# A decoder layer with experts: a 21st weight buffer, and single buffers for gathered rows and for a pair's result

## What is computed

```python
g_w, g_idx = lax.top_k(g_prob, 1)
e_w, e_idx = lax.top_k(e_prob, TOP_K_IN_GROUP)
w = e_w / jnp.sum(e_w, axis=-1, keepdims=True) * g_w
for e in range(N_EXPERTS):
    h = jax.nn.silu(xt @ lp['w_e_gate'][e]) * (xt @ lp['w_e_up'][e])
    y = y + combine[:, e:e + 1] * (h @ lp['w_e_down'][e])
```

## Time and profile before

| | |
|---|---|
| median of 3 runs | 804.66 us (803.05 to 805.99) |
| the profiled execution's own time | 804.41 us |
| its span, first to last instruction | 802.3 us |
| PE busy | 757.4 us (94%) |
| DVE, ACT, POOL busy | 390.1, 244.0, 74.5 us |
| DMA | 190.64 MB, mean 238 GB/s |
| chain that ended last | PE 76%, DMA 14%, ACT 5%, DVE 3% |

### The profile page before, as it was taken

The page is one execution under the profiler, slowest core; times in us unless marked ns, Lnnn a source line. Parts: engine busy times, 40 slices in busy tenths (PEclk is TensorE's granted clock), DMA queues, the critical chain, the costliest instruction groups (busy, mean ns, idle before and its releaser), DMA issues.

```text
span 802.3 us, 12106 instructions
## 1 busy us (share of the span) xinstructions
PE 757.4 (94%) x4992; PEld 577.7 (72%) x4992; DVE 390.1 (49%) x733; ACT 244.0 (30%) x429; POOL 74.5 (9%) x104
## 2 busy tenths in 40 slices
PE   8999999999999999999999999999999997788884
PEld 6889999999998766789999989887333332333322
DVE  3599828994632747466344358446111111113227
ACT  1552333213473435553243243112111110110113
POOL 0100022001003010100000010002112112111100
PEclk9999999999999999999999999999999999999998
DMA  9668134623345454210242378269999999999995
GB/s 343 239 179 336 60 112 79 153 68 151 93 152 209 187 210 158 106 54 2 105 139 86 158 299 340 99 218 384 398 417 427 419 420 427 420 422 426 421 398 190
DMA packets 38140, 190.64 MB, mean 238 GB/s; under 512 B 5914, under 2 KB 7466, under 8 KB 21864
## 3 DMA queue, kind: packets, MB, share of 16 engines
q1 hardware_dynamic: 23696, 148.22, 46.8%
q0 software_dynamic: 11200, 34.98, 13.1%
q10 hardware_dynamic: 3184, 6.60, 2.2%
HBM read 176.17 MB, written 21.41 MB: 246 GB/s over the span
## 4 chain that ended last, share of the span: by engine, by line
PE 76%; DMA 14%; ACT 5%; DVE 3%; issue 1%; SPq 1%; DVEq 0%; ACTq 0%; POOLq 0%
PE ps L619 72%; DMA sb<-in_wexp 10%; PE ps L630 4%; DMA expert_rows<-sb 2%; DMA sb<-expert_rows 1%; ACT sb L1522 1%; ACT sb L1451 1%; DMA sb<-in_xT 1%; SPq L519 1%; ACT sb L1323 1%; ACT sr L1438 0%; DVE sb L2559 0%; ACT sb L1500 0%; DVE sb L2059 0%; DVE sr L2032 0%
## 5 line engine op out<-in xcount | busy, mean ns | idle before, releaser
L619 PE MATMUL ps<-sb 128*64 128x512 f32 (+15 forms) x2208 | 383.4, 434 | 29.2 <-DMA sb<-in_wexp 17.9
L619 PE MATMUL ps<-sr 128*128 128x288 f32 (+2 forms) x2378 | 337.0, 302 | 3.5 <-DVE sr L2502 1.6
L619 PEld LDWEIGHTS ps<-sb 128*64 128x64 f32 (+6 forms) x2208 | 217.9, 157 | 167.4 <-issue 130.1
L619 PEld LDWEIGHTS ps<-sr 128*128 128x128 f32 x2378 | 319.9, 188 | 15.8 <-issue 5.1
L630 PEld LDWEIGHTS ps<-sb 128*128 128x128 f32 (+3 forms) x406 | 41.8, 140 | 32.1 <-issue 28.9
L2428 DVE SCALAR_TENSOR_TENSOR sb<-sb,ps 128x256 f32<-128x256 f32 x16 | 6.7, 421 | 116.6 <-ACT sb L1690 116.6
L630 PE MATMUL ps<-sb 128*128 128x128 f32 (+3 forms) x406 | 52.9, 269 | 3.3 <-issue 1.7
L2167 DVE TENSOR_TENSOR sr<-sb,sr 128x2048 fp32r<-128x2048 f32 (+1 forms) x15 | 34.7, 2324 | 27.4 <-ACT sr L1433 17.6
L2436 DVE COPY sb<-ps 128x1024 f32<-128x1024 f32 x15 | 18.4, 1225 | 57.6 <-PE ps L619 57.6
L1323 ACT ACTIVATE sb<-ps 128x576 f32<-128x576 f32 (+4 forms) x29 | 22.9, 790 | 70.3 <-PE ps L619 50.4
L2153 DVE SCALAR_TENSOR_TENSOR sb<-sb,ps 128x576 f32<-128x576 f32 x24 | 18.1, 753 | 53.3 <-PE ps L619 53.3
(11 more groups left out here) (279 smaller groups left out, 482.7 us busy)
## 6 DMA issues: line engine op xcount, KB each, us to landing
sb<-in_wexp SPq DMA_DIRECT2D x91, 1024.0 KB, 22.0
sb<-in_wstream SPq DMA_DIRECT2D x33, 1024.0 KB, 5.3
expert_rows<-sb ACTq DMA_DIRECT2D x1, 4608.0 KB, 20.1
sb<-in_mkT POOLq DMA_DIRECT2D x8, 512.0 KB, 8.8
sb<-in_mv POOLq DMA_DIRECT2D x8, 512.0 KB, 6.4
sb<-expert_rows SPq DMA_DIRECT2D x4, 1024.0 KB, 9.5
sb<-in_wexp SPq DMA_DIRECT2D x5, 768.0 KB, 24.9
sb<-in_x SPq DMA_DIRECT2D x4, 512.0 KB, 14.4
```

What stands on the lines that cost most here:

```text
L619: return signed(nc.tensor.matmul(*a, **kw))
```

## The change

1. **A 21st slot.** It is put in ahead of the last one and has two pieces of half a chunk each, so a chunk that goes there is two transfers: `M_YO + 1024`, until now the second result buffer, and `M_XG + 1024`, until now the second buffer of gathered rows. Chunk n goes to slot n modulo 21; from chunk 21 on it waits for chunk n - 21. Since an odd number of slots no longer falls into pairs, the semaphores are a ring of their own (`EW_RING`, 11).
2. **Order on SP.** Chunk 19, now in the new slot, is started behind chunk 18 and before the wait for the stores of `xn2_rows`; it waits for logits of the fourth row block (`lg3`), which have read the place before. Chunk 20 goes behind that wait.
3. **One buffer of gathered rows.** gather(i) waits until turn_rows(i-1) is done, where before it waited for turn_rows(i-2).
4. **One result buffer.** result(i) waits until scatter(i-1) has landed, where before it waited for scatter(i-2).
5. **The last result.** `L_HI` and `L_SEL` move to the places of slots 13 and 12. ACT drops its wait for a scatter, DVE's wait for turned rows becomes one for `ew_used`.

```diff
-SLOTS_E += [straight(O_X)]
+SLOTS_E += [[(M_YO + 1024, ((1, 1024),), 0, 1024), (M_XG + 1024, ((1, 1024),), 1024, 1024)], straight(O_X)]
+EW_RING = 11
 def landed(n):
 
-    k = n % NSLOT // 2 * 2
-    return 16 * (len(SLOTS_E[k]) + len(SLOTS_E[k + 1])) * (n // NSLOT + 1)
+    pairs = range(n // 2 % EW_RING, n // 2 + 1, EW_RING)
+    return 16 * sum(len(SLOTS_E[2 * m % NSLOT]) + len(SLOTS_E[(2 * m + 1) % NSLOT]) for m in pairs)
...
-L_HI, L_LO, L_SEL, L_W = M_YO + 1024, M_XGT, M_XG + 1024, R_SS + 13
+L_HI, L_LO, L_SEL, L_W = SLOTS_E[13][0][0], M_XGT, SLOTS_E[12][0][0], R_SS + 13
...
-                    sp.dma_start(at(off, *dims), src).then_inc(ew_ready[n % NSLOT // 2], 16)
+                    sp.dma_start(at(off, *dims), src).then_inc(ew_ready[n // 2 % EW_RING], 16)
...
             for n in range(15, 19):
                 main_chunk(n)
+            filled(sp, f"lg{TT - 2}")
+            main_chunk(19)
             sp.wait_ge(x2_out[0], 48)
             sp.wait_ge(x2_out[1], 32)
-            for n in range(19, N_MAIN):
+            for n in range(20, N_MAIN):
                 wait_pos(sp, ew_used, n + 1 - NSLOT)
...
-                    last = turn_tile(pat(0, kt * 128, (1, 128)), at(M_XG + (i % 2) * 1024 + kt * 128, (1, 128)), ident)
+                    last = turn_tile(pat(0, kt * 128, (1, 128)), at(M_XG + kt * 128, (1, 128)), ident)
...
             act.wait_ge(slot_oh, 3)
-            act.wait_ge(y_sent[1], 16 * (NPAIR // 2 - 1))
...
                 dve.wait_ge(y_ps, i + 1)
-                wait_pos(dve, y_sent[i % 2], 16 * (i // 2))
-                v.tensor_copy(at(M_YO + (i % 2) * 1024, (1, 1024)), pat(3, 0, (1, 1024))).then_inc(y_copied, 1)
+                if i:
+                    dve.wait_ge(y_sent[(i - 1) % 2], 16 * ((i + 1) // 2))
+                v.tensor_copy(at(M_YO, (1, 1024)), pat(3, 0, (1, 1024))).then_inc(y_copied, 1)
...
-                dve.wait_ge(xt_ps, NPAIR)
+                dve.wait_ge(ew_used, N_MAIN - NSLOT + 2)
...
-                wait_pos(pool, xt_ps, i - 1)
+                if i > 1:
+                    pool.wait_ge(xt_ps, i)
                 pool.indirect_dma_start(
-                    out=at(M_XG + (i % 2) * 1024, (1, D)), out_offset=None, in_=x2_d[:, :],
+                    out=at(M_XG, (1, D)), out_offset=None, in_=x2_d[:, :],
```

More of the change, by code:

```diff
@@ L163 @@
 SLOTS_E += [straight(a) for b in (0, 2) for a in (raw_at(NBLOCKS - 4 + b), raw_at(NBLOCKS - 3 + b), HI_AT["w", b], HI_AT["w", b + 1])]
-SLOTS_E += [straight(O_X)]
+SLOTS_E += [[(M_YO + 1024, ((1, 1024),), 0, 1024), (M_XG + 1024, ((1, 1024),), 1024, 1024)], straight(O_X)]
 NSLOT = len(SLOTS_E)
-assert NSLOT == 20 and O_XH + 3584 <= WORDS and O_X + 4096 <= O_TH
+EW_RING = 11
+assert NSLOT == 21 and NSLOT <= 2 * EW_RING - 1 and O_XH + 3584 <= WORDS and O_X + 4096 <= O_TH
 def piece_of(n, i):
@@ L420, in build @@
         x2_out = [sem(f"x2_out{i}") for i in range(2)]
-        ew_ready = [sem(f"ew_ready{i}") for i in range(NSLOT // 2)]
+        ew_ready = [sem(f"ew_ready{i}") for i in range(EW_RING)]
         ew_used = sem("ew_used")
@@ L573, in _ @@
                 sp.wait_ge(added, 1)
+                sp.wait_ge(y_lo, 2)
                 for n in range(N_MAIN, len(CHUNKS)):
@@ L1116, in weights_of @@
                 if n % 2 == 0:
-                    pe.wait_ge(ew_ready[n % NSLOT // 2], landed(n))
+                    pe.wait_ge(ew_ready[n // 2 % EW_RING], landed(n))
                 return n
@@ L2683, in scatter @@
                     out=y_d[:, :], out_offset=bass.IndirectOffsetOnAxis(at(M_IDX + i, (1, 1)).bitcast(U32), 0),
-                    in_=at(M_YO + (i % 2) * 1024, (1, D)), in_offset=None,
+                    in_=at(M_YO, (1, D)), in_offset=None,
                     bounds_check=PAIRS - 1, oob_is_err=False).then_inc(y_sent[i % 2], 16)
```

## The result

The changed kernel takes 807.14 us as a median of 22 runs (806.07 to 812.76), the kernel before 804.64 us in as many on the same chip. The ratio is 1.0035 with a 95% interval from 1.0026 to 1.0044: **slower, by 2.5 us between the medians and 2.8 us by the ratio**, where 0.9 us less was forecast, and above the range's end of 806.8. The profiled execution takes 807.03 us (span 805.2).

What follows compares the result with a forecast made beforehand. The stream of weights was taken to bound the kernel. The slot's -2.0 us and the result buffer's +1.1 us, with nothing for the other parts, gave -0.9 us: from 804.66 to 803.8 us, range 802.0 to 806.8.

Steps and rivals of the forecast that it cites:

- Part 1, the slot: Chunk 19 starts near 542 us and fills the DMA hole at 555 to 570 us: gain 2.0 us (1.3 to 2.5).
- bytes or busy share: Two measures of the hole at 555 to 570 us: missing bytes give 2.7 us, the DMA engines' empty share 1.3.
- Part 2, the rows: At the experts' start, turn_rows(1) and (2) come 2.0 and 3.1 us later, hidden by queued weights; the end not later.
- The cover: At the experts' start, about 3.5 us remain before the weights' queue runs dry, against a PE delay of 3.1 us.
- Part 3, the result buffer: At the end, result(14) waits for scatter(13), 5.6 us later, so the loads of the results end 1.1 us later.
- (a): At the end, scatter(14) starts loaded and ends alone: 5.0 us, landing at 775.1.
- (b): Behind scatter(14), the first load of the results, 1024 KB alone, takes 4.8 us instead of 6.4, landing at 779.9.
- (c): From the landing of scatter(14), a chain without slack runs to the end; no change in its length was forecast.
- The rival on the slower side: At the end, scatter(14) is as slow as under load, deciding from 5.9 us: +1.9 us, 806.6 or 807.3; chance 0.15.
- That rows bind: Rival: the single buffer of rows costs PE 3.1 us at the start or up to 12.8: 806.9 to 816.6; chance 0.05.
- That the tail is free: Rival: at the end scatter(14) lands within about 3.9 us, so loads wait for DMA alone: 802.4 us; chance 0.18.
- Released after 776: Sign of error at the end: the loads of the results are released after 776 us.

Runs made afterwards that it cites:

- the two experiments without the slot: Kernel before with one result buffer alone: 809.31 us, ratio 1.0057; kernel before with one buffer of gathered rows alone: 804.35 us, ratio 1.000.
- the kernel with the own place: Changed kernel, but result(14) goes to a place of its own in a used weight slot, without waiting: 802.94 us, ratio 0.9968; again 802.61 and 802.83 us.
- the last experiment: Six spare products on PE before turn_rows(1), added to the kernel with the own place: 806.09 us, ratio 1.0026.

## Why the prediction was wrong

- **Part 1, the slot: right, in mechanism and about in size.** The step taken as 2.0 measured 2.5 in the profiled execution, in two more of the changed kernel 1.4 and 2.9. The last is more than one chunk can give, so these marks move by themselves; the two experiments without the slot have 200.8 and 201.3 in place of 201.6. The medians of the kernel with the own place, which keeps the slot and the single buffer of rows, give 1.5 to 1.8 us: 2.0 was rather a little high, and whether bytes or busy share (1.3) was the better measure stays open.
- **Part 2, the rows: right in sum, the steps differ from execution to execution.** Late by 2 and 3 us was forecast, 0 and 0.9 came in the profiled execution, and alone the single buffer changed nothing (ratio 1.000). Gather(2) landed after 8.7 us, as forecast (8.8), but gather(1) in at most 6.1 (turn_rows(1) stands that far behind it), so that the delay did not begin with it. In the ten profiled executions with the early chunk 19 and nothing else changed at this place, turn_rows(1) came 7.0 to 10.2 us after the first product, where it was 7.4 before: the 2.0 us happen, but not always. The cover, taken as some 3.5 us, is rather 2 by the last experiment. What the single buffer costs beside the slot, where gathers meet a full queue, no run shows by itself.
- **Part 3, the result buffer: the right place, three sizes off, all to the same side. This is the step that failed.** (a) scatter(14) was to start loaded and end alone, 5.0 us; it took 6.44, on DMA engines that moved 14 GB/s at the end. A free queue did not make it fast: its last packets were late although little else was under way. By the fit of the Trainium skill (DMA: Bandwidth & Descriptors, Anatomy of one DMA — SWDGE (gpsimd) path) 3.2 us would have done, as an estimate; the fastest scatter(14) in any run, by the time from its start to the loads that wait for it, took 5.9. (b) The first load was to take 4.8 us alone, because the 6.4 of before were put down to the last chunk ahead of it. With nothing ahead of it, it took 6.2, and 6.1 to 6.3 in the nine other profiled executions with a late result(14). The row it was priced by the earlier trace rows is a transfer with none behind it; behind the first load come four more, and the engines had moved some 1.9 MB when its 1.05 had landed. That this is what made it late is argued; no run started it alone. With result(14) late by 5.3 us in place of 5.6, these two are 2.6 us. (c) "From there a chain without slack runs to the end" was taken as a chain of unchanged length. It grew by 2.3 us in the profiled execution, by 1.1 and 2.5 in two more of the changed kernel, since weights that came earlier and loads that came later left PE idle, and at half clock around and behind that.
- **The rival on the slower side** had the place right, and a scatter(14) above the 5.9 us from which it was to decide, though not as slow as under load. It was given 0.15 because "half of its time falls after the last weights". That its price, 3.9 us, is near the 3.7 that came by the landing of the first load is luck: it was made of a scatter of 7.8 us and a load of 4.8, where 6.44 and 6.2 were measured. So is the time near its 807.3, which had a gain of 1.3 us in it and no longer end. **That rows bind** fell as the cause of the loss: ratio 1.000 alone, and the loss is gone with the own place, which keeps the single buffer of rows. **That the tail is free** fell with the 6.44 us. The rule of two buffers (the Trainium skill, Trainium Kernel Development and Optimization, Best Practices) is borne out at the results, 4.7 us, and not at the rows.
- **Released after 776** was named as a sign of error; the release came at 773.3, and the prediction was wrong all the same, since two later steps were.

What stays open: the clock's share in the median (0.2 to 1.4 us), and how often the slot's gain is lost between 565 and 580 us. That scatter(14) is slow because single DMA engines finish late is argued from the few packets at the end; no run changed that alone, and none started the first load without the others.

## What to carry to other kernels

When a second buffer is given up, look for the place where two uses of it follow more closely than in the steady loop: here a distance of 12 us hid a landing of 8 us in every pair but the last, and that one was on the end's own chain. Keep the buffer there alone: the 21st slot with a place of its own for one result is 0.2 to 0.3% faster than the kernel before (three sets of runs; the interval of one reaches 1.0007) and some 0.6% faster than the change. And price a transfer at the end by the nearest transfer of its own kind, with what is started behind it as well as what stands ahead, and ask what the engines behind it do while it is waited for.

## What had not been expected of the hardware

- In all six profiled executions in which PE stood idle for 3.7 to 5.9 us near the end, the granted clock was at 0.50 around or behind it. With 0.5, 1.6 and 1.9 us it stayed up, with 1.5 and 2.2 us it fell, in one execution each. A wait of 1.43 us ahead of the last down products stands in all eighteen profiled executions; within 2 us behind it the clock fell in ten and stayed up in eight. At such lengths it goes either way.
- A scatter of 128 rows (512 KB) that had the DMA engines nearly to itself for its last 2 us still took 6.44 us, against 7.8 and 8.6 beside the weights. In the ten profiled executions with a late result(14) it took 5.9 to 6.6 us.
- A queue that is full in the middle does not forget its start: 1 MB started 14 us earlier gave back 2.5 us at result(13), 200 us later, in the profiled execution (1.5 to 1.8 us of the whole time by the medians with the own place), and PE being 5 us late at the start put 3.3 us on the end.
